# The second mixer of a two-block network rebuilt as one stage: one weight stream, token-major values, broadcast decay rows

## What is computed

```python
h  = rmsnorm(x,   g) * (1 + sc_m) + sh_m          # 256 tokens
hc = rmsnorm(ctx, g) * (1 + sc_c) + sh_c          # 256 context tokens
na_k, na_v, ml_k, ml_v, ml_g, na_q, ml_q, ml_o, gate_na, gate_ml = split(h @ w_in)
na_kc, na_vc, ml_kc, ml_vc, ml_gc = split(hc @ w_in[:, :N_CTX_COLS])
o_na = neighbourhood_attention(na_q, na_k, na_v, na_kc, na_vc, rpb)   # 8 heads of 64
o_ml = mlstm_branch(...)                          # 4 heads, keys 64, values 128, both directions
merged = sigmoid(gate_na) * (o_na @ w_branch_na) + sigmoid(gate_ml) * (o_ml @ w_branch_ml)
x = x + gt_m * rmsnorm(merged @ w_out, g_post)
```

## Time and profile before

| | us |
|---|---|
| median of 3 runs (2958.86 to 2969.26) | 2962.99 |
| the profiled execution, its own time | 2967.32 |
| its span (first to last instruction) | 2965.6 |
| TensorE busy in the span | 2588.9 (87%) |
| DVE busy | 1288.0 (43%) |
| ACT busy | 851.1 (29%) |
| GpSimd busy | 43.4 (1%) |
| mean granted TensorE clock | 0.951 of 2.4 GHz |

### The profile page before, as it was taken

One profiled execution on the slowest core, in us unless ns is written; L12 is line 12 of the kernel. 1 busy time (PEld: TensorE's weight loads), 2 busy tenths in 40 slices (PEclk: granted clock), 3 DMA queues, 4 the chain that ended last, 5 costly groups with the idle time before them and its releaser, 6 DMA issues. The chain is left out here.

```text
span 2965.6 us, 35139 instructions
## 1 busy us (share of the span) xinstructions
PE 2588.9 (87%) x13196; PEld 1729.1 (58%) x13197; DVE 1288.0 (43%) x2045; ACT 851.1 (29%) x1349; POOL 43.4 (1%) x61
## 2 busy tenths in 40 slices
PE   4998999897998999898699697679888988889887
PEld 2887898786787988687589365523322323223232
DVE  2655755664654755564313765452212212121122
ACT  3344444443444444443324321201100001000011
POOL 0000000000000000000000000200000000000000
PEclk9999999998999999999789797789999999999999
DMA  6753343763753444673224110569999999999994
GB/s 223 262 183 132 126 132 115 262 227 134 253 198 134 149 129 135 218 244 116 74 69 149 29 57 1 201 263 409 410 410 409 410 410 410 410 410 410 410 362 184
DMA packets 185902, 686.99 MB, mean 232 GB/s; under 512 B 20530, under 2 KB 21938, under 8 KB 184530
## 3 DMA queue, kind: packets, MB, share of 16 engines
q1 hardware_dynamic: 177860, 650.95, 59.0%
q0 software_dynamic: 7488, 29.36, 2.8%
q10 hardware_dynamic: 432, 5.08, 0.4%
HBM read 683.24 MB, written 2.11 MB: 231 GB/s over the span
## 5 line engine op out<-in xcount | busy, mean ns | idle before, releaser
L2083 PE MATMUL ps<-wexp_all_second,con_all_whole 128*64 128x512 f32 x3168 | 706.5, 596 | 69.6 <-DMA wexp_all_second<-in_w_lin 69.6
L2083 PEld LDWEIGHTS ps<-wexp_all_second,con_all_whole 128*64 128x64 f32 x3168 | 218.7, 137 | 514.9 <-issue 378.5
L561 DVE TENSOR_TENSOR lo_first<-raw_first,hi_first 128x1024 fp32r<-128x1024 f32 x264 | 308.7, 1221 | 40.6 <-ACT hi_first L531 40.4
L241 PE MATMUL ps<-hi_first,h_hi_first 128*128 128x512 f32 x704 | 286.1, 406 | 21.7 <-DVE lo_first L561 21.7
L243 PE MATMUL ps<-hi_first,h_lo_first 128*128 128x512 f32 x704 | 281.0, 399 | 0.0
L242 PE MATMUL ps<-lo_first,h_hi_first 128*128 128x512 f32 x704 | 280.7, 399 | 0.0
L531 ACT CAST hi_first<-raw_first 128x1024 fp32r<-128x1024 f32 x264 | 260.5, 1055 | 19.1 <-DMA raw_first<-in_ffn_wgu 19.1
L241 PE MATMUL ps<-h_hi_first,w_hi_first 128*128 128x256 f32 x848 | 249.2, 294 | 2.2 <-DVE w_lo_first L1006 2.2
L242 PE MATMUL ps<-h_lo_first,w_hi_first 128*128 128x256 f32 x848 | 240.6, 284 | 0.0
L243 PE MATMUL ps<-h_hi_first,w_lo_first 128*128 128x256 f32 x848 | 240.5, 284 | 0.0
L1006 DVE TENSOR_TENSOR w_lo_first<-raw_first,w_hi_first 128x1024 fp32r<-128x1024 f32 x122 | 148.7, 1223 | 158.4 <-ACT w_hi_first L917 157.9
(11 more groups left out here) (382 smaller groups left out, 3595.0 us busy)
## 6 DMA issues: line engine op xcount, KB each, us to landing
wexp_all_second<-in_w_gate SPq DMA_DIRECT2D x64, 2048.0 KB, 23.3
wexp_all_second<-in_w_lin SPq DMA_DIRECT2D x64, 2048.0 KB, 23.9
wexp_all_second<-in_w_down SPq DMA_DIRECT2D x64, 2048.0 KB, 22.1
raw_first<-in_ffn_wgu SPq DMA_DIRECT2D x176, 512.0 KB, 4.9
raw_first<-in_w_mix SPq DMA_DIRECT2D x138, 512.0 KB, 3.4
raw_first<-in_ffn_wd SPq DMA_DIRECT2D x88, 512.0 KB, 5.0
wada_first<-in_w_ada POOLq DMA_DIRECT2D x48, 512.0 KB, 4.6
raw_second<-in_w_g SPq DMA_DIRECT2D x16, 512.0 KB, 4.2
```

Of the source, the lines that this page charges most:

```text
L241: nc.tensor.matmul(out, w_hi, x_hi, start=start, stop=False, skip_group_check=True)
L561: nc.vector.tensor_tensor(lo[:, slot], raw[:, slot], hi[:, slot].bitcast(F32), ALU.subtract).then_inc(s[f"{kind}_lo"], 1)
L2083: mm = nc.tensor.matmul(dst[side(half), :], lhs(k), B.wexp[2 * "gld".index(kind) + part][:, k % 4, half * HALF:(half + 1) * HALF], start=( ...
```

## The change

All phases of the second mixer become one, `mixer2_program`. Removed are `load2_phase`, `norm_pair_phase`, `kv_phase`, `plain_project_phase`, `prepare2_phase`, `attention_phase`, `mlstm_phase`, `head_norm_phase`, `merge_phase`, `out_phase` and their helpers.

- One weight stream `w_mix2` of 57 chunks on SP: 41 input chunks in the order of `UNITS2`, 8 branch chunks, 8 output chunks; ring of 4 raw and 3 split slots. The context is normalised between the first chunks. The 32 table loads are issued behind the loads of chunks 2 to 9, the bias tables' loads and the router's behind all chunks.
- Values are projected token-major (tokens as weights, 512 columns of `w_in` moving, four banks accumulated over four chunks), so that their transposes and copies go. The 16 gate columns are one padded chunk and four small transposes.
- Near units use the `Attention` class; units sit between half chunks (chunks 12 to 20, closing to 22), with one output bank; the output is divided, token-major, and turned back once (8 transposes).
- The decay of a key no longer depends on the query but for a constant: 8 rows (4 heads x 2 directions) x 512 keys are formed once (`decays`), cut into three bf16 parts on DVE (`decay_parts`), and each recurrent unit broadcasts its row with one or two bf16 products and adds the mask with another (`Mlstm`). Keys outside the mask are left out where a whole block of 128 is (half of the units). The row's own constant enters in the lower bound (`own_decay`). Recurrent units sit in two of three half chunks (chunks 24 to 37).
- The merge has four product banks; the gain rows are made between output chunks; sigmoid of the merge gates is done beside the branch products.

Core of the diff (added lines; `mixer_program` and `moe_phase` keep their text):

```diff
+    def pe_scores(self, pe, u):
+        nc, B, (h, qc, d) = self.nc, self.B, self.units[u]
+        lo, row = (h % 2) * HD, d * ML_HEADS + h
+        if u >= 2:
+            pe.wait_ge(self.s["l_exp"], u - 1)
+        at = 0
+        for a, b in self.runs(u):
+            nc.tensor.matmul(self.decay(u)[:, at:at + b - a], B.pick8[:, row:row + 1].broadcast_to([3 * E, P]), B.decay3[:, a:b],
+                             start=(at == 0), stop=False, skip_group_check=True)
+            at += b - a
+        diag = P if (qc, d) == (1, 0) else 0
+        nc.tensor.matmul(self.decay(u)[:, diag:diag + P], B.ident16, B.mask16[:, d, :], start=False, stop=True, skip_group_check=True)
+        if u >= 2:
+            pe.wait_ge(self.s["l_gated"], u - 1)
+        at = 0
+        for a, b in self.runs(u):
+            mm = nc.tensor.matmul(self.score(u)[:, at:at + b - a], B.q10[lo:lo + HD, MLQ + h // 2, qc * P:(qc + 1) * P],
+                                  B.kv[lo:lo + HD, MLK + h // 2, a:b], start=(at == 0), stop=True, skip_group_check=True)
+            at += b - a
+        mm.then_inc(self.s["l_scores"], 1)
...
+    def dve_gate(self, dve, ch, u):
+        dve.wait_ge(self.s["l_exp"], u + 1)
+        p, den = self.prob(u), self.stat(u, 1)
+        self.nc.vector.scalar_tensor_tensor(p, p, 1.0, self.score(u)[:, 0:self.width(u)], ALU.mult, ALU.mult,
+                                            accum_out=den).then_inc(self.s["l_gated"], 1)
+        dve.wait_ge(self.s["l_gated"], u + 1)
+        ch.link(self.nc.vector.scalar_tensor_tensor(den, den, -1.0, den, ALU.mult, ALU.max))
+        ch.link(self.nc.vector.tensor_scalar(den, den, self.stat(u, 2), None, ALU.max))
+        self.nc.vector.reciprocal(self.stat(u, 3), den).then_inc(self.s["l_recip"], 1)
...
+UNITS2 = ([("x", NAQ + j) for j in range(4)] + [("x", MLQ + j) for j in range(2)] + [("all", NAK + j) for j in range(4)]
+          + [("v", (NAV, j)) for j in range(4)] + [("gates", 0)] + [("all", MLK + j) for j in range(2)] + [("x", MLO)]
+          + [("v", (MLV, j)) for j in range(4)] + [("x", MLO + j) for j in range(1, 4)] + [("g", j) for j in range(G2)])
...
+NEAR_SLOTS, ML_SLOTS = {}, {}
+_j = 0
+for _c in range(V_NEAR + 2, N_IN2):
+    for _half in range(2):
+        if (_c, _half) >= (V_NEAR + 2, 1) and _j < NA_HEADS * TC + 3 and (UNITS2[_c][0] != "x" or _half == 0):
+            NEAR_SLOTS[_c, _half] = _j
+            _j += 1
+for _j in range(2 * TC * ML_HEADS + 3):
+    _h = 2 * ML_FIRST + (3 * _j) // 2
+    ML_SLOTS[_h // 2, _h % 2] = _j
...
+            sp.dma_start(B.vec2, I["vec2"]).then_inc(s["vec_in"], 16)
+            load(0)
+            sp.dma_start(B.ctx, I["ctx"]).then_inc(s["ctx_in"], 16)
+            for c in range(1, N_MIX2):
+                load(c)
+                if 2 <= c < 2 + NA_HEADS:
+                    table_rows(c - 2)
+            sp.dma_start(B.w_r, I["w_router"]).then_inc(s["r_in"], 16)
+            sp.wait_ge(s["near_ready"], TC)
+            sp.wait_ge(s["decay_out"], 2)
+            sp.wait_ge(s["prod"], 1)
+            bias_table_sp(sp, s, B, I)
+            sp.wait_ge(s["r_in"], 16)
...
+            def half_unit(c, half):
+                kind, which = UNITS2[c]
+                r = c % SPLIT
+                if half == 0:
+                    pe.wait_ge(s["lo"], c + 1)
+                if kind == "v":
+                    if half == 0 and which[1] == 0:
+                        pe.wait_ge(s["out"], outs_before(c))
+                        pe.wait_ge(s["rope_done"], 2 if c == V_NEAR else 4)
+                        if c == V_ML:
+                            pe.wait_ge(s["g_in"], 1)
+                    for t in (2 * half, 2 * half + 1):
+                        for j in range(2):
+                            k = 2 * which[1] + j
+                            w, tok = slice(j * HALF, (j + 1) * HALF), slice(t * P, (t + 1) * P)
+                            mm = product(nc, ps[:, t, :], B.h_hi[:, k, tok], B.h_lo[:, k, tok], B.w_hi[:, r, w], B.w_lo[:, r, w],
+                                         k == 0, k == KD - 1)
+                        if which[1] == 3:
+                            mm.then_inc(s["v_done"], 1)
+                    if which[1] == 3:
+                        return
+                else:
+                    n = T if kind in "xg" else NT2
+                    if half == 0 and c >= 2:
+                        pe.wait_ge(s["out"], bank_free(c))
+                    for k in range(4 * half, 4 * half + 4):
+                        if c in (0, NAK_AT):
+                            pe.wait_ge(s["h_lo_done"], k + 1 + (KD if c else 0))
+                        w = slice(k * P, (k + 1) * P)
+                        mm = product(nc, bank(c)[:, 0:n], B.w_hi[:, r, w], B.w_lo[:, r, w], B.h_hi[:, k, 0:n], B.h_lo[:, k, 0:n],
+                                     k == 0, k == KD - 1)
+                if half == 1:
+                    mm.then_inc(s["mm"], 1)
...
+                rows = ps[0:3 * E, 2, :]
+                after, before = con("after"), con("before")
+                one = dict(stop=False, skip_group_check=True)
+                mm = nc.tensor.matmul
+                for t in range(KT):
+                    mm(rows[:, t * P:(t + 1) * P], B.g_li[:, t, :], con("ident"), start=(t == 0), **one)
+                mm(rows[:, 0:P], B.g_f[:, 0, :], after[:, 0, 0:P], start=False, **one)
+                mm(rows[:, T:NT2], B.g_f[:, 0, :], after[:, 0, T:NT2], start=False, **one)
...
+            def ml_close(j):
+                if 2 <= j < n_ml + 2:
+                    if j == 2:
+                        pe.wait_ge(s["near_ready"], TC)
+                    lstm.pe_turn(pe, j - 2)
+                if j >= 3:
+                    lstm.pe_values(pe, j - 3)
...
+            for c in range(N_IN2):
+                for half in range(2):
+                    near, ml = NEAR_SLOTS.get((c, half)), ML_SLOTS.get((c, half))
+                    if near is not None:
+                        near_open(near)
+                    if ml is not None:
+                        ml_open(ml)
+                    half_unit(c, half)
+                    if near is not None:
+                        near_close(near)
+                    if ml is not None:
+                        ml_close(ml)
+                if c == 1:
+                    pe.wait_ge(s["x_scaled"], 2)
+                    pe.wait_ge(s["odd_scaled"], 2)
+                    pe.wait_ge(s["h_ready"], KD)
+                    turn_pe(nc, s, B, B.xs[:, 2:4, :], x_bank)
...
+            pe.wait_ge(s["out"], outs_before(N_IN2))
+            for k in range(KD):
+                pe.wait_ge(s["lo"], N_IN2 + k + 1)
+                pe.wait_ge(s["m_lo"], k + 1)
+                for t in range(TC):
+                    mm = tile(k, t)
+                    if k == KD - 1:
+                        mm.then_inc(s["acc_done"], 1)
+                if k < KD - 1:
+                    mm.then_inc(s["mm"], 1)
+                if k == 2:
+                    pe.wait_ge(s["merged"], KD)
+                    gain_row(0)
+                    gain_row(1)
+                if k == 5:
+                    gain_row(2)
+                    gain_row(3)
...
+            def constants():
+                ch.did(nc.vector.tensor_copy(B.ident16, con("ident")))
+                ch.did(nc.vector.tensor_copy(B.mask16[:, 0, :], con("causal")[:, 0, 0:P]))
+                ch.did(nc.vector.tensor_copy(B.mask16[:, 1, :], con("anticausal")[:, 0, 0:P]))
+                ch.did(nc.vector.tensor_copy(B.pick8, con("thrice")[0:3 * E, 0:2 * ML_HEADS]))
...
+            scale_odd(0)
+            modulation()
+            lower(0)
+            halves(0, KD)
+            lower(1)
+            for c in range(N_IN2):
+                if c + 2 < N_IN2:
+                    lower(c + 2)
+                if c == 0:
+                    scale_odd(1)
+                if c in (1, 2):
+                    halves(KD + 4 * (c - 1), 4)
...
+                    if ml is not None:
+                        if ml < n_ml:
+                            lstm.dve_max(dve, ml)
+                        if 1 <= ml < n_ml + 1:
+                            lstm.dve_gate(dve, ch, ml - 1)
+                        if ml >= 3:
+                            lstm.dve_add(dve, ch, ml - 3)
...
+    values = lambda at: w[:, at:at + 4 * P].reshape(KD // 2, 2, P, 4 * P).transpose(0, 2, 1, 3).reshape(4, P, D)
...
```

More of the change, by code:

```diff
@@ new lines, in near_units, with scores @@
+def near_units(nc, B):
+    units = []
+    for h in range(NA_HEADS):
+        lo = (h % 2) * HD
+        for qc in range(TC):
+            def scores(dst, h=h, lo=lo, qc=qc):
+                return nc.tensor.matmul(dst, B.q10[lo:lo + HD, NAQ + h // 2, qc * P:(qc + 1) * P],
+                                        B.kv[lo:lo + HD, NAK + h // 2, :], start=True, stop=True)
+            units.append(dict(scores=scores, table=B.na_table[:, h * TC + qc, :], sink=None,
```

(26 more changed lines are left out.)

1181 lines of the change are left out of this document (543 added, 638 removed).

## The result

| | us |
|---|---|
| kernel before, median of 4 runs (2958.86 to 2969.26) | 2963.93 |
| changed kernel, median of 4 runs (2797.65 to 2802.72) | 2800.16 |
| ratio, with 95% interval | 0.9445 [0.9433, 0.9457] |
| profiled execution, its own time / its span | 2798.76 / 2797.1 |
| second mixer, from the first load of its vector to the first expert weight | 330.25 (before 496.9) |

The change saves 164 us; 2799 stood in the prediction. In the two profiled executions the spans differ by 168.5 us: 166.6 is the mixer, 2 lie ahead of it (it began at 1402.95 instead of 1404.94 us), and the rest behind it is as long as it was, 1063.8 us in both.

What follows compares the result with a forecast made beforehand. TensorE's queue was taken to bound the second mixer: 302 us of work + 20 head + 10 waits + 2 barriers + 1 tail = 335 for 498, a gain of 163, giving 2799 us; range 2775 to 2852.

Steps and rivals of the forecast that it cites:

- GpSimd tie: End of the second mixer: GpSimd's bias-table chain ends at 29.6 us, TensorE at 30; 1 us added.
- waits inside: TensorE's waits inside the second mixer, among them near values 1 us, key rope 2, decay rows 1; 10 us in all.
- Projections: TensorE's projection chunks: 26 over 256 tokens at 2.83 us and 15 over 512 at 5.45; 155 us.
- Near units: 16 near-attention units on TensorE, 2.38 us each with values at 0.74; 38 us.
- Recurrent units: 16 recurrent units on TensorE, 2.5 us each with the new decay products at 0.35; 40 us (35 to 46).
- Head: Start of the second mixer, loading and normalising: 20 us for the present 39, its six projections counted elsewhere.
- GpSimd ends the stage: Rival at the mixer's end: late loads make GpSimd's chain late, +5 to 8 us, 2804 to 2807 us; 8%.
- SP's 32 table transfers: Table transfers between the loads of chunks 2 to 9: cost nothing, or 3 us if one load is late.
- Exposed chains: Rival in the 32 units: TensorE waits 3.1 us in half of them, +50 us, 2849; in all, 2899; 16%.
- Everything meets: Rival for the whole mixer: no lateness or waits, low bounds of the decay products; 25 us less, 2774 us; 8%.
- Half clock: Rival in chunks 12 to 37: TensorE runs at 1.2 GHz; 3101 us if all work does; 2%.
- It does not do what it says: Part of the forecast: units are not hidden between chunks; gain from decay 43 us, gates 11, idle stretches about 100.

## Why the prediction was right, point by point

| step of the sum | forecast | measured |
|---|---|---|
| head with six projections | 20 + 17 | 35.7 |
| chunks 6 to 22, near units, turns | 128.6 | 133.2 |
| decay rows, chunk 23, near back | 8.8 | 9.0 |
| chunks 24 to 37, recurrent units | 79.6 | 81.1 |
| last three chunks, back transposes | 9.5 | 9.6 |
| branch products | 28 | 27.4 |
| output, GpSimd tie, barriers | 30 + 3 | 34.3 |
| waits inside | 10 | in the rows above |
| sum | 335 | 330.3 |

(The recurrent units begin at 1580.76 us.) The sum is some 4 us off in 330. Part of that closeness is luck: 8 us too much for the waits inside (10 against 2.0) stand against some 4 too little for all the rest, 2.6 of it in the chunks with near units, 1.5 in those with recurrent units and 1.3 at the output, less 1.3 in the head.

- **Projections.** Half a chunk between two units takes 2.87 us, not 2.72: the first product behind a unit costs some 0.1 us more. I had left out that price of alternating; over the 35 or so halves it is an estimated 3 to 4 us.
- **Near units.** 2.42 us each against 2.38. Two terms inside it were wrong and nearly cancel, which is luck: values with 64 columns moving take 0.93 us, not 0.74 (I had scaled by instruction count), and scores with transposes take 1.49 us, not 1.64. Eight value products take 0.93 us ahead of scores with 64 columns, 0.98 with 128, and 0.82 with 64 where no scores follow.
- **Recurrent units.** (81.1 - 14 x 2.83) / 16 = 2.6 against 2.5 us. The decay, for which no row stood, took 0.38 us for a full unit and 0.32 for a shortened one; 0.35 was taken. The 2.72 us that went is the cheaper of two kinds of unit; half of them had 0.96 us more, so the decay's 43 us in the split should have been 16 x 2.72 + 8 x 0.96, or 51. The sum of 335 does not use it.
- **Waits inside** was the largest miss: 2.0 us (key rope 1.3, near values 0.7) where 10 stood. Behind the decay rows TensorE did not wait, and nothing like the 6 us carried over from the first mixer, where 4.5 were waits for ACT's copies, came back; why they are absent no run shows.
- **Head.** 18.7 against 20 us, and at the places named: 5.3 us to the first transposes and 4.4 for them, unit 0 3.3 us longer, then 1.7 us of waiting for the context, 1.7 for its transposes and 1.5 for a weight half.
- **GpSimd tie.** Called a tie at +1; it costs 3 to 5 us. Its chain ended 30.6 us behind the last branch product, where 29.6 was forecast, and TensorE 33.1, where 30 was: in part through the stall of DVE and the clock behind it, neither of which the prediction had. The rival "GpSimd ends the stage" came true in the kernel with one more reduction.
- **SP's 32 table transfers** cost nothing: no wait of TensorE in the mixer is for a transfer.
- **Exposed chains.** No unit waited; DVE had 0.7 us a unit to give without loss and not 2.07.
- **Everything meets** (2774) did not come: its low end left out alternation and the tie, though its waits were nearly gone. Its 25 us are not the sum of what it names either (6, 6, 10 and 5.6 for the decays make 27.6, and one 6 lies within the 10). By its own terms the forecast is 2800 and not 2799 us (2804.3 - 4.3), and half of the units waiting gives 2849, not the 2852 of the range.
- **Half clock.** I took 0.97 of the earlier trace rows as proof that small products keep the clock. The number was right and the reason was not: the chunk halves keep it. Bare, the near units in the new form ran at 0.50. The risk that I priced at 2% stood one reordering away.
- **What the clock gave.** The prediction sums at full clock and names decay, gates and idle stretches as the sources of the gain. An estimated 29 us of it are TensorE's work going at 2.4 GHz instead of 1.2, and this source it does not name.
- **"It does not do what it says."** That units between chunks are not hidden is shown (38.5 of 39 us). The split of the gain is not: cheaper products are worth 11 of 37 us in the old order, 48 of 50 in the new.

## What to carry to other kernels

Where one engine is busy all the time, forecast by its queue and measure every shape of instruction in it; here a tenth of a microsecond had to be added for each change from a unit's products back to the projections. A wait of TensorE can cost more than its own length: behind waits of 1.8 and 2.9 us six products went at half clock. Before units with few moving columns are run back to back, look at the granted clock: wide products between them, or unused columns, were worth more here than the work that they add. Before work is put on GpSimd, look at the longest, not the mean, of DVE's instructions with two SBUF operands beside it.

## What the runs showed of the hardware that I had not expected

- TensorE almost without pauses (66.3 of 67.0 us) at half clock for 67 us with 64 columns moving in its values, and back at 2.4 GHz within 7 us with 128.
- Waits of 1.8 to 2.9 us behind which TensorE ran six to nine products of 512 columns at half clock, another 1.2 to 1.7 us.
- DVE subtractions of 1.23 and 0.43 us that took 4.3 and 4.2 us beside a subtraction of GpSimd.
- Eight value products take nearly the same with 64 moving columns (0.93 us) as with 128 (0.98).
- With near units or part of the decays left out of the mixer, the part behind it takes 14 and 11.6 us longer.
